# A streamed weight load of one decoder layer: two units per DMA instead of one

## The reference

```python
h = rms_norm(x, g_mix_pre)
proj = h @ w_in                       # q,k,v | z,xBC,dt | short conv | 3 gates
y_attn = moba_attention(q, k, v, rel_bias)        # one block: causal, 8 heads of 128
y_ssm  = mamba2_mixer(z, xbc, dt_raw, ...)        # 32 heads of 64, 4 groups
y_sc   = sc_b * causal_depthwise_conv(sc_c * sc_h)
merged = g_a*(y_attn @ w_br_attn) + g_m*(y_ssm @ w_br_ssm) + g_c*(y_sc @ w_br_conv)
x = x + rms_norm(merged @ w_out, g_mix_post)
u = square(relu(rms_norm(x, g_mlp_pre) @ w_mlp_up))
x = x + rms_norm(u @ w_mlp_down, g_mlp_post)
gate = sigmoid(rms_norm(x, g_ple_pre) @ w_ple_gate)
x = x + rms_norm(gate * (p @ w_ple_proj), g_ple_post)
```

## Time and profile before

| | us |
|---|---|
| median of 3 runs | 1896.39 |
| the profiled execution, its own time | 1895.98 |
| its span in the profile | 1894.4 |
| TensorE busy | 1881.2 |
| VectorE busy | 1158.6 |
| ScalarE busy | 944.9 |
| POOL busy | 50.5 |

### The profile page before, as it was taken

The page is one execution under the profiler, slowest core; times in us unless marked ns, Lnnn a source line. Parts: engine busy times, 40 slices in busy tenths (PEclk is TensorE's granted clock), DMA queues, the critical chain, the costliest instruction groups (busy, mean ns, idle before and its releaser), DMA issues.

```text
span 1894.4 us, 27093 instructions
## 1 busy us (share of the span) xinstructions
PE 1881.2 (99%) x9554; PEld 1595.8 (84%) x9554; DVE 1158.6 (61%) x1296; ACT 944.9 (50%) x1140; POOL 50.5 (3%) x101
## 2 busy tenths in 40 slices
PE   9999999999999999999999999999999999999998
PEld 8888888888888888888888888888888888888886
DVE  7645555565656777765555676556555655665675
ACT  6544455545445666654444564344434443444564
POOL 1000000000000000000000000100000000000010
PEclk9999999999999999999999999999999999999999
DMA  7665555665555755555565566555555555556554
GB/s 254 223 219 177 176 177 177 209 212 195 193 190 176 235 177 187 167 179 188 189 211 193 172 208 217 196 184 195 189 196 189 191 189 192 188 185 189 177 190 144
DMA packets 100094, 364.62 MB, mean 192 GB/s; under 512 B 11561, under 2 KB 11705, under 8 KB 99609
## 3 DMA queue, kind: packets, MB, share of 16 engines
q1 hardware_dynamic: 96912, 351.32, 55.7%
q0 software_dynamic: 2960, 12.36, 1.9%
q10 hardware_dynamic: 160, 0.11, 0.0%
HBM read 361.60 MB, written 3.70 MB: 193 GB/s over the span
## 4 chain that ended last, share of the span: by engine, by line
PE 99%; ACT 0%; DVE 0%; issue 0%; DVEq 0%; POOL 0%; ACTq 0%; POOLq 0%
PE ps L1455 28%; PE ps L1477 18%; PE ps L1479 18%; PE ps L1478 18%; PE ps L1459 14%; PE ps L1652 0%; PE ps L1502 0%; PE ps L1624 0%; PE ps L1718 0%; PE ps L1654 0%; PE ps L1673 0%; PE ps L1641 0%; PE ps L1552 0%; PE ps L1563 0%; PE ps L1558 0%; DVE w_lo L737 0%
## 5 line engine op out<-in xcount | busy, mean ns | idle before, releaser
L737 DVE TENSOR_TENSOR w_lo<-w_raw,w_hi 128x1024 fp32r<-128x1024 f32 x661 | 807.4, 1228 | 600.3 <-ACT w_hi L334 597.2
L334 ACT ACTIVATE w_hi<-w_raw 128x1024 fp32r<-128x1024 f32 x661 | 693.1, 1057 | 696.0 <-PE ps L1479 484.3
L1455 PE MATMUL ps<-act,w_hi 128*128 128x512 f32 x2320 | 733.8, 397 | 1.7 <-DVE w_lo L737 1.0
L1477 PE MATMUL ps<-w_hi,act 128*128 128x512 f32 x1340 | 522.9, 390 | 0.8 <-DVE act L1174 0.8
L1459 PEld LDWEIGHTS ps<-act,w_lo 128*128 128x128 f32 x2320 | 435.8, 188 | 102.0
L1479 PE MATMUL ps<-w_hi,act 128*128 128x512 f32 x1340 | 521.5, 389 | 0.0
L1478 PE MATMUL ps<-w_lo,act 128*128 128x512 f32 x1340 | 521.4, 389 | 0.0
L1459 PE MATMUL ps<-act,w_lo 128*128 128x256 f32 x2320 | 457.4, 278 | 0.0
L1455 PEld LDWEIGHTS ps<-act,w_hi 128*128 128x128 f32 x2320 | 355.0, 189 | 4.8 <-issue 2.8
L1477 PEld LDWEIGHTS ps<-w_hi,act 128*128 128x128 f32 x1340 | 251.5, 188 | 53.5 <-issue 1.3
L1479 PEld LDWEIGHTS ps<-w_hi,act 128*128 128x128 f32 x1340 | 251.5, 188 | 52.7
(11 more groups left out here) (232 smaller groups left out, 849.9 us busy)
## 6 DMA issues: line engine op xcount, KB each, us to landing
w_raw<-w_stream SPq DMA_DIRECT2D x662, 512.0 KB, 3.4
a_rows<-decay_rows POOLq DMA_DIRECT2D x8, 512.0 KB, 6.3
x_tok<-x_tok_in POOLq DMA_DIRECT2D x4, 512.0 KB, 5.7
x_T<-x_in SPq DMA_DIRECT2D x3, 512.0 KB, 9.9
out<-x_tok SPq DMA_DIRECT2D x3, 512.0 KB, 2.7
bias<-bias_rows POOLq DMA_DIRECT2D x8, 128.0 KB, 3.2
gain_mix<-gains_in POOLq DMA_DIRECT2D x1, 1024.0 KB, 6.3
gain_mlp<-gains_in POOLq DMA_DIRECT2D x1, 1024.0 KB, 7.3
```

Source lines behind the costliest of these rows:

```text
L334: act.activation(whi[:, s, :], raw[:, s, :], ACT.Copy).then_inc(hi_ready, 1)
L737: dve.tensor_tensor(wlo[:, s, :], raw[:, s, :], whi[:, s, :], ALU.subtract)\
L1455: pe.matmul(bank[2 * g + t], whi[:, s, at_:at_ + P], a.rearrange("p a t -> p (a t)"), start=first and i == 0, stop=False)
L1477: pe.matmul(out_, hi, whi[:, s, n], start=first and i == 0, stop=False)
```

## The change

From unit 4 on, one DMA loads two units, n and n + 1 (n even), from two neighbouring places of `wstream` into two neighbouring slots. It waits until the lo of both slots' old units is made, and raises the semaphore of the even slot alone. ScalarE waits on the even slot's semaphore for both units; for the first four units it waits on each one's own, as before.

```diff
             with sp.Fori(1, UNITS // SLOTS) as it:
-                for s in range(SLOTS):
-
-                    sp.wait_ge(lo_ready, it * SLOTS + (s + 1 - SLOTS))
-                    sp.dma_start(raw[:, s, :], wstream[ds(it * SLOTS + s, 1)]
-                                 .rearrange("o p n -> (o p) n")).then_inc(w_loaded[s], 16)
-            for n in range(UNITS // SLOTS * SLOTS, UNITS):
-                sp.wait_ge(lo_ready, n + 1 - SLOTS)
-                sp.dma_start(raw[:, n % SLOTS, :], wstream[n]).then_inc(w_loaded[n % SLOTS], 16)
+                for s in range(0, SLOTS, 2):
+
+                    sp.wait_ge(lo_ready, it * SLOTS + (s + 2 - SLOTS))
+                    sp.dma_start(raw[:, s:s + 2, :], wstream[ds(it * SLOTS + s, 2)]
+                                 .rearrange("o p n -> p o n")).then_inc(w_loaded[s], 16)
+            for n in range(UNITS // SLOTS * SLOTS, UNITS, 2):
+                s = n % SLOTS
+                sp.wait_ge(lo_ready, n + 2 - SLOTS)
+                sp.dma_start(raw[:, s:s + 2, :], wstream[n:n + 2].rearrange("o p n -> p o n"))\
+                  .then_inc(w_loaded[s], 16)
...
             def split_hi(e, c):
 
                 s = c % SLOTS
-                act.wait_ge(w_loaded[s], e * 4 + 16 * (c // SLOTS + 1))
+                if isinstance(e, int) and e + c < SLOTS:
+                    act.wait_ge(w_loaded[s], 16)
+                else:
+                    act.wait_ge(w_loaded[s // 2 * 2], e * 4 + 16 * (c // SLOTS + 1))
```

## The result

The changed kernel takes **1905.38 us** (median of 6 runs, 1902.51 to 1905.83) against 1896.37 us for the kernel before (6 runs, 1896.00 to 1896.52): a ratio of 1.0046 with a 95% interval of 1.0035 to 1.0056. It is slower by 9.0 us where 3.1 were forecast, and the time lies outside the forecast range of 1897.0 to 1905. The profiled execution took 1905.17 us, with a span of 1903.6.

The account below looks back on a forecast made before the run. TensorE was taken to bound the kernel, loads costing only where it waits. Start 2.3 plus unit 643 0.8 gave 3.1 us on the profiled 1895.98, 1899.1; with the runs' median 0.4 above, 1899.5; range 1897.0 to 1905.

Parts of the forecast that it names:

- What bounds the kernel: Whole kernel: TensorE, busy 1881.2 of 1894.4 us, sets the end; a load counts only where it makes TensorE wait.
- Everywhere else: nothing: Outside the start and unit 643: even units' hi 1 to 2 us late, covered by TensorE's reserve; no loss.
- X: Landing time of a 1 MB pair load, taken as 4.6 us, between 3.8 and 5.4.
- The upper bound of 5.4: Highest landing time assumed for 1 MB: two loads issued 1.14 us apart are both there after 5.4 us.
- Step 1: Start, units 4 to 19: late pair loads delay TensorE 2.3 us, unit 4's 1 us stall included; bounds 0.7 and 3.9.
- Step 2: Unit 643, last stage's first sigmoids: pair 642/643 makes hi 642 1.5 us late, costing 0.8 us; bounds 0 and 2.3.
- the forecast relief: Unit 643: lo 643, past POOL's products, gets 1.0 us shorter; lo 642 1.1 longer, mostly covered by VectorE's 0.8 idle.
- Rival A: Up projections become load-bound once landing reaches 5.0 us, TensorE stalling from 5.4: about 1908 us; chance 0.12.
- a pair has no neighbour in flight here: Up projections: argument against load-bound blocks, as a lone pair is issued 3 us before the next.
- Rival B: Start and unit 643 dearer (landing 4.9 to 5.4 us, or no VectorE relief): 3.8 to 7 us, 1900 to 1903.5; chance 0.25.
- idle time between 66 and 1790 us: Sign that would prove the forecast wrong: TensorE idle anywhere in that stretch.
- ScalarE's copies starting later than TensorE allows: Up projections: sign that would prove the forecast wrong, ScalarE's copies delayed beyond TensorE's release.

Follow-up runs that it names:

- run 1: Kernel before, own 512 KB loads, but the even unit's load also waits for its neighbour's remainder: 1896.41 us, ratio 1.0002.
- run 3: Changed kernel with pair loads only for units 4 to 375, own loads from unit 376 on: 1900.83 us, ratio 1.0024.
- run 4: Changed kernel, all pairs; in the up projections VectorE makes the block's sum and square ahead of the fourth unit's lo: 1902.18 us, ratio 1.0030.
- run 5: Changed kernel, all pairs; VectorE makes lo 630 behind the sums of the last down block: 1906.17 us, ratio 1.0051.
- run 6: Changed kernel with own loads for units 4 to 7 too, pairs from unit 8: 1907.74 us, ratio 1.0058.
- run 7: Changed kernel with weights laid out so a pair is one 8 KB row per partition, not two of 4 KB: 1904.22 us, ratio 1.0037.
- run 8: Changed kernel with pairs from unit 24 and VectorE's sums ahead of lo in up projections and ahead of lo 630: 1899.46 us, ratio 1.0016.
- run 11: Kernel before with one more unused VectorE subtract ahead of lo 19, no pair loads: 1897.84 us, ratio 1.0011.
- run 12: Kernel before with two more unused VectorE subtracts ahead of lo 19, no pair loads: 1900.35 us, ratio 1.0023.
- run 2: Changed kernel with own loads for units 0 to 23 and pairs from unit 24: 1902.75 us, ratio 1.0036.

## Why the prediction was wrong, step by step

**What bounds the kernel** held: TensorE, with isolated places without reserve. The two steps that were named came near their size, the second of them by luck; the failure lies in the sentence "Everywhere else: nothing".

**X** was 4.8 us (4.69 for pair 8/9, 4.88 for 12/13), not 4.6: a small miss. The upper bound of 5.4 was the time of two loads with a gap between them; back to back they need 4.56 (run 1). In the start X scatters: pair 12/13 took up to 5.47 us in runs 3 to 6.

**Step 1, the start:** 2.3 us forecast, 2.3 measured (1.05 + 1.28), with hi 4, hi 8 and hi 12 at 18.36, 26.71 and 36.64 us (forecast 18.7, 26.9, 36.5), from ScalarE's timeline:

```profile
18.36 2.01 ACT L339 ACTIVATE w_hi<-w_raw 128x1024 fp32r<-128x1024 f32 x2 [2.09 <-DMA w_raw<-w_stream]
...
26.71 1.06 ACT L339 ACTIVATE w_hi<-w_raw 128x1024 fp32r<-128x1024 f32 x1 [0.46 <-DMA w_raw<-w_stream]
...
36.64 1.06 ACT L339 ACTIVATE w_hi<-w_raw 128x1024 fp32r<-128x1024 f32 x1 [3.20 <-DMA w_raw<-w_stream]
```

With X of 4.69 and 4.88 in place of twice 4.6 the sum gives 2.7; the chain absorbed 0.4. That the stall at unit 4 is part of it and not added is shown by the same trace: lo 19 comes 2.29 us later than before, and TensorE behind it is 2.28 late. That the size hit so well is partly luck: in runs 3, 4 and 5, with the same loads, the waits of the start cost 3.0 to 3.3 us, in the main because pair 12/13 landed later. There, and in run 6, the wait for lo 19 was 2.65 us and a further 1.5 us of slow products followed, which the prediction had no term for.

**Step 2, unit 643:** 0.8 forecast, 0.6 measured, but not by the forecast way. VectorE in the changed kernel, then its lo 642 in run 4:

```profile
1835.01 2.63 DVE L1308 TENSOR_TENSOR rowbuf<-ev,emb 128x512 f32<-128x512 f32 x2 [0.78 <-ACT ev L687]
...
1839.79 3.45 DVE L742 TENSOR_TENSOR w_lo<-w_raw,w_hi 128x1024 fp32r<-128x1024 f32 x2
```

```profile
1830.22 2.20 DVE L742 TENSOR_TENSOR w_lo<-w_raw,w_hi 128x1024 fp32r<-128x1024 f32 x1 [2.48 <-ACT w_hi L339]
```

The late hi 642 was right in kind (1.1 us later than before, TensorE's own delay taken off, where 1.5 were forecast). But lo 643 did not become shorter and lo 642 not longer; the first two products beside POOL took 2.63 us instead of the 3.16 of the earlier trace rows, and that is the relief. In runs 4, 5, 7 and 8 the forecast relief did come (lo 643 took 1.2 us, lo 642 1.7 to 2.3), and there the step was 1.1. So the late load and the path to unit 643 were right, the account with POOL's products was not, and the 0.8 is close by luck.

**The up projections: the step that failed.** The prediction compared a loop of X + 6.2 us with 11.16 and found the threshold at X = 5.0. The measured loop is 11.54 with X = 4.85, so X + 6.7. The half microsecond left out is VectorE's lo of the late unit itself. I had let ScalarE's copy start the rest of the loop from the place it had before; but hi 458 makes lo 458 possible at 1320.07, and VectorE's order puts this lo *ahead* of the block's sum, which starts at 1321.21 instead of right behind the copy. The threshold was X = 4.5, below my own forecast of 4.6. Rival A was thus the case, with a wrong condition; its effect per block is 0.4 us, against a reserve of 3.3, so it shows as 0.3 to 0.4 us once behind the up projections of each later quarter, and as 1.7 in the first. Run 4, in which VectorE makes the sum ahead of this lo and nothing else differs, shows it: the five steps go. The argument against Rival A, that a pair has no neighbour in flight here, did not hold either: in the block above the next pair is issued 2.3 us later, well before the first has landed.

**The turn: a place not looked at.** I priced the unit where the earlier trace rows shows a stall and the one where POOL gets in the way, and did not ask, stage by stage, which engine's order puts a lo ahead of a sum that TensorE needs. The trace of before had the sign: of the 3.8 us that TensorE idles ahead of its end, 0.8 is a wait at 1794.66 us, at unit 630, beside the one of 1.0 that I named. At unit 630 VectorE's order does put a lo ahead of such a sum, and the lateness from the up projections arrives there unspent: 2.0 us of waiting more than before. That it is handed on is shown by run 4 (3.5 to 0.24 us), that the order decides where it hits by run 5.

**TensorE's clock: a term that no step had.** 1.5 us of the 3.5 at the turn. Each stall was priced at its own length; that slow products can follow a hole was in no sum. The rows of before show the clock at 1.00 in the stretch of the short stall, and gave no case of a longer one.

In the sum, for the profiled execution: 3.1 forecast; the same two places 2.9; up projections 2.8; turn 2.0; clock 1.5. Together 9.2. Rival B (the same places, dearer), the one I gave most weight on the slow side, was not the cause.

Of what the prediction would have taken as proof it was wrong, two signs came: idle time between 66 and 1790 us, and ScalarE's copies starting later than TensorE allows.

The Trainium skill (DMA: Bandwidth & Descriptors, Bandwidth) asks for 1 MB or more per DMA, to reach 75% or more of the peak bandwidth. The trace agrees in direction (the same 351.3 MB kept the queue busy for 52.6% of the span instead of 55.7), and no place here turned that into time: the first half of the weights came 1.5 us later instead (run 1).

## What to carry to other kernels

Merging two loads makes the first half as late as the second. Before merging, write out the loop of every stage from issue to issue with *all* instructions that the in-order engines put between landing and release, at the new landing time, and compare it with the time that the bound engine needs; where the two are within half a microsecond, count the blocks against the reserve and follow what is left into the next stage. Look for places where an engine's order puts work that waits for a load ahead of work that doesn't, and allow for a hole of over 2 us in TensorE's work costing more than its length: here mostly about 1.5 us more, but not each time. A size that was met in one execution is not yet met: the same code cost 2.8 to 4.3 us in the up projections by the execution.

## What the runs showed of the hardware that I had not expected

- **TensorE's granted clock can fall behind a hole of some 2.3 to 3.5 us**, to 0.53 to 0.66 in the mean of the next stretch of 3 us (products 0.43 us apart instead of 0.227), which costs about 1.5 us on top (the step at the unit less what the wait grew: 3.21 - 1.64 in run 3, 2.81 - 1.26 in run 11, 3.97 - 2.51 in run 12). It did so behind 3.52 us (run 12), 2.65 (runs 3 to 6), 2.27 (run 11), and at the turn behind two holes with eight short transposes between them: 1.82 + 0.86 (the changed kernel), 1.86 + 0.86 (run 6) and 2.29 + 0.86 (run 2). It did not behind 2.28 us at 63 us in the changed kernel, nor behind 2.65 us in run 7, where TensorE had had three more short waits between 26 and 52 us, nor behind 0.98 + 0.86 at the turn (run 7), 1.61 (run 5) or 1.71 (run 8). So the length of the hole alone does not decide it, and what else does stays open. The two groups of runs in run 11, whose means are 2 us apart (1897.4 and 1899.4), go with this (the mean granted clock is 0.997 in the one and 0.998 in the other). The 1902.5 among the 1905s of the changed kernel may be the same; no profile of it shows that.
- **Two 512 KB loads issued back to back are both there before one of 1 MB**: 4.56 against 4.8 us, the first at 3.27. With half the rows (run 7) the 1 MB load still took 4.8 us.
- **The landing of one and the same load scatters enough to move a stall.** Pair 12/13 took 4.88 us in the changed kernel's profile and 5.25 to 5.47 in runs 3 to 6; the wait for lo 19 went from 2.28 to 2.65 us with it, and in those four the slow products followed. Run 6, with two pair loads fewer, measured 1907.74 us against 1905.38, and its profile has this longer wait and the slow products; runs 3 to 5 have them too, with all the start's pairs, so fewer pairs are not shown to be slower.
